# Attention stages of a two-model layer stack: turns one step behind the scores in two of three kinds of attention

## What is computed

```python
def diff_core(q, k, v, lam):                     # two maps a head, subtracted
    s = einsum('bqhid,bkhid->bhiqk', q, k) * DA ** -0.5
    p = softmax(s, axis=-1)
    w = p[:, :, 0] - lam * p[:, :, 1]
    return einsum('bhqk,bkhd->bqhd', w, v)

def mla_core(qn, qr, kn, kr, v):                 # scores are a sum of two products
    s = (einsum('bqhd,bkhd->bhqk', qn, kn) + einsum('bqhd,bkd->bhqk', qr, kr)) * MLA_SCALE
    return einsum('bhqk,bkhd->bqhd', softmax(s), v)

# window_gqa: scores of 256 context keys and of a band of up to 3 x 128 keys, softmax with a sink
# nsa_mixer: per query block o_c * gate_c + o_s * gate_s + o_w * gate_w, each a masked softmax @ values;
#   (31 compressed keys; selected keys; a window)
```

## Time and profile before

| | |
|---|---|
| median of 3 runs | 4268.4 us (4262.95 to 4271.06) |
| the profiled execution | 4266.7 us; its span 4264.5 us |
| PE busy | 3891.0 us, 91% |
| DVE busy | 2230.9 us, 52% |
| ACT busy | 1583.4 us, 37% |
| the eight attention calls together | 709.4 us (sum of their windows) |
| the six that are not combined | 553.0 us |

### The profile page before, as it was taken

One profiled execution on the slowest core, in us unless ns is written; L12 is line 12 of the kernel. 1 busy time (PEld: TensorE's weight loads), 2 busy tenths in 40 slices (PEclk: granted clock), 3 DMA queues, 4 the chain that ended last, 5 costly groups with the idle time before them and its releaser, 6 DMA issues. The chain is left out here.

```text
span 4264.5 us, 53701 instructions
## 1 busy us (share of the span) xinstructions
PE 3891.0 (91%) x19922; PEld 3027.8 (71%) x19922; DVE 2230.9 (52%) x3880; ACT 1583.4 (37%) x2699; POOL 318.7 (7%) x282
## 2 busy tenths in 40 slices
PE   4998979997999898999899899979889998988998
PEld 3875557776888787865666688856568886657886
DVE  6346567854553574364522556255555525565552
ACT  2235561112442453254611344243434424343431
POOL 0000001111000000100000100104010010401001
PEclk8999989998999999999999999989799999979999
DMA  4100005551222343100022233222023322202322
GB/s 173 57 31 19 1 17 175 195 185 54 96 96 100 107 163 114 65 23 19 1 83 86 79 97 97 95 71 80 11 79 95 102 89 85 75 21 79 98 98 80
DMA packets 86728, 350.82 MB, mean 82 GB/s; under 512 B 9520, under 2 KB 9648, under 8 KB 85680
## 3 DMA queue, kind: packets, MB, share of 16 engines
q1 hardware_dynamic: 72752, 298.53, 21.3%
q0 software_dynamic: 13824, 50.34, 3.5%
HBM read 346.73 MB, written 2.10 MB: 82 GB/s over the span
## 5 line engine op out<-in xcount | busy, mean ns | idle before, releaser
L493 DVE TENSOR_TENSOR split_low<-weight_ring,split_high 128x1024 fp32r<-128x1024 f32 (+1 forms) x456 | 606.2, 1330 | 893.3 <-ACT split_high L485 878.3
L485 ACT ACTIVATE split_high<-weight_ring 128x1024 fp32r<-128x1024 f32 (+1 forms) x474 | 524.7, 1109 | 1037.8 <-PE banks L1342 469.3
L1470 PE MATMUL banks<-normed_high,split_high 128*128 128x512 f32 (+1 forms) x1760 | 653.6, 371 | 77.9 <-DVE normed_low L432 37.9
L1470 PE MATMUL banks<-normed_low,split_high 128*128 128x512 f32 (+1 forms) x1760 | 651.2, 370 | 0.0
L1470 PE MATMUL banks<-normed_high,split_low 128*128 128x512 f32 (+1 forms) x1760 | 650.4, 370 | 0.0
L1470 PEld LDWEIGHTS banks<-normed_high,split_high 128*128 128x128 f32 x1760 | 334.4, 190 | 139.8 <-issue 83.6
L1470 PEld LDWEIGHTS banks<-normed_low,split_high 128*128 128x128 f32 x1760 | 334.5, 190 | 55.6
L1470 PEld LDWEIGHTS banks<-normed_high,split_low 128*128 128x128 f32 x1760 | 334.4, 190 | 55.2
L1342 PE MATMUL banks<-hidden_high,split_high 128*128 128x512 f32 (+1 forms) x880 | 325.1, 369 | 7.2 <-DVE split_low L493 7.2
L1342 PE MATMUL banks<-hidden_high,split_low 128*128 128x512 f32 (+1 forms) x880 | 324.4, 369 | 0.0
L1342 PE MATMUL banks<-hidden_low,split_high 128*128 128x512 f32 (+1 forms) x880 | 324.3, 369 | 0.0
(11 more groups left out here) (301 smaller groups left out, 6641.6 us busy)
## 6 DMA issues: line engine op xcount, KB each, us to landing
weight_ring<-in_up SPq DMA_DIRECT2D x220, 512.0 KB, 3.5
weight_ring<-in_down SPq DMA_DIRECT2D x80, 704.0 KB, 4.0
modulation_ring<-in_ada POOLq DMA_DIRECT2D x80, 512.0 KB, 4.5
weight_ring<-in_merge SPq DMA_DIRECT2D x48, 768.0 KB, 4.5
weight_ring<-in_inputs SPq DMA_DIRECT2D x36, 512.0 KB, 3.5
weight_ring<-in_out SPq DMA_DIRECT2D x32, 512.0 KB, 3.5
latents<-in_ada POOLq DMA_DIRECT2D x16, 512.0 KB, 4.6
weight_ring<-in_xbc SPq DMA_DIRECT2D x16, 512.0 KB, 3.6
```

What stands on the lines that cost most here:

```text
L485: act.activation(k.splits[0][:, (n0 + panel) % RING, 0:width], k.slot(n0 + panel)[:, 0:width], ACT.Copy).then_inc(k.high_ready.sem, 1)
L493: dve.tensor_tensor(k.splits[1][:, s, 0:width], k.ring[:, s, 0:width], k.splits[0][:, s, 0:width].bitcast(F32), ALU.subtract).then_inc(k.l ...
L1470: last = pe.matmul(sums(r, half), w, x, start=(c + j == 0), stop=(c == KT - 1 and j == 2))
```

## The change

`behind` is 2 for a combined call and 1 for the others. Where it is 2, nothing changes. Where it is 1:

- PE issues in iteration t: score(t), turn(t-1, 0), weigh(t-2), turn(t-1, 1).
- ACT issues: copy(t-1, 0), both exponentials of t, copy(t-1, 1).
- DVE issues: normalise(t-1) of both maps, then both maxima of t, then store(t-2).
- Each loop has one iteration less.

No instruction is added or taken away, and no buffer, bank or DMA is changed.

```diff
+    behind = 2 if combined else 1
...
-            for t in range(U + 3):
+            for t in range(U + behind + 1):
                 if t < U:
                     score(t)
-                if 2 <= t < U + 2:
-                    turn(t - 2, 0)
-                if t >= 3:
-                    weigh(t - 3)
-                if 2 <= t < U + 2 and per == 2:
-                    turn(t - 2, 1)
+                if behind <= t < U + behind:
+                    turn(t - behind, 0)
+                if t > behind:
+                    weigh(t - behind - 1)
+                if behind <= t < U + behind and per == 2:
+                    turn(t - behind, 1)
...
-            for t in range(U + 3):
+            def normalise_both(t):
+                if 0 <= t < U:
+                    normalise(t, 0)
+                    normalise(t, 1)
+
+            for t in range(U + behind + 1):
+                if behind == 1:
+                    normalise_both(t - 1)
                 if t < U:
                     maximum(t, 0)
                     maximum(t, 1)
-                if 1 <= t <= U:
-                    normalise(t - 1, 0)
-                    normalise(t - 1, 1)
-                if t >= 3:
-                    store(t - 3)
+                if behind == 2:
+                    normalise_both(t - 1)
+                if t > behind:
+                    store(t - behind - 1)
...
-            for t in range(U + 2):
-                if t >= 2:
-                    copy(t - 2, 0)
+            for t in range(U + behind):
+                if t >= behind:
+                    copy(t - behind, 0)
                 if t < U:
                     exponential(t, 0)
                     exponential(t, 1)
-                if t >= 2 and per == 2:
-                    copy(t - 2, 1)
+                if t >= behind and per == 2:
+                    copy(t - behind, 1)
```

## The result

The changed kernel takes 4242.6 us (median of 4 runs, 4238.85 to 4244.40), the kernel before took 4268.65 in the runs beside it (4262.95 to 4271.06). The ratio is 0.9939, with a 95% interval of 0.9924 to 0.9955: faster by 26 us, 0.6%. Forecast were 4255.2 and a range of 4246 to 4266. The sign was right, the size (13.2 us) was half of what came, and the time lies 3.4 us under the lower end.

What follows compares the result with a forecast made beforehand. PE was taken to bound latent calls, three engines with waits window calls, PE at clock 0.71 sparse calls. Latent -6.4, window -4.2, sparse +0.8, clock -3.4: -13.2 us, giving 4255.2 us, range 4246 to 4266.

Steps and rivals of the forecast that it cites:

- The prediction's own sign of being wrong: Wrong if the clock moved by over 13 us either way in these calls or the stages behind them.
- Drain: End of a call: one round of turn and weigh goes, saving 4.1 us latent, 3.2 and 3.6 window, 2.5 sparse.
- Fill: Start of a call: turn pair fills PE's 2.02 us hole, costing 0.9 us latent, 1.3 window, 1.3 sparse.
- Middle of the window calls: Loop through DVE and ACT stays 0.24 us a step shorter than what binds already: no cost.
- Order of the sparse calls: Drain -2.5, fill +1.3, DVE loop +1.6 a call (2.6 at full clock): +0.8 us for both calls.
- Clock of the first model: Latent and window calls: 12.8 us lost at half clock, a quarter regained by filling the second hole: -3.4 us.
- Clock of the sparse calls: No gain forecast; half of PE's load was called clock, and slow stretches only hid loop cost, 1.6 instead of 2.6 us.
- The combined calls: The two calls whose order is not changed were to stay at 89 and 67 us.
- Case 3: The clock doesn't fall at the start of calls: -22.6 us, 4245.8 us; chance 0.15.
- Case 2: DVE's order takes back the clock gain, full 2.6 us loss per sparse call: 4260 to 4265 us; chance 0.24.
- Case 4: Slower: the new loop's holes before scores keep PE at 1.2 GHz in window calls: 4280 us; chance 0.06.
- The rule of the Trainium skill: PE idling briefly and often between matmul groups oscillates between clock levels; a loop every step would cost more than its holes.

Runs made afterwards that it cites:

- fill_small_before: Kernel before, old order, plus unused 128x256 products behind score(0) and score(1) in latent, window and combined calls: 4251.75 us, ratio 0.9963.
- both_mixed: As both_after, but sparse calls keep the old order (turns two steps behind, maxima first): 4236.8 us, ratio 0.9930.
- both_after: Changed kernel plus unused products behind score(0) in latent, window and combined calls, and at several places in the sparse calls: 4235.3 us, ratio 0.9926.
- keep_before: Kernel before, old order, plus unused 128x256 products in the two sparse calls alone, 29 a call: 4256.6 us, ratio 0.9975.
- window_only: Kernel before with the new order in the two window calls alone, no products: 4257.0 us, ratio 0.9974.
- latent_only: Kernel before with the new order in the two latent calls alone, no products: 4259.7 us, ratio 0.9984.
- normalise_first: Changed kernel with turns two steps behind again in all calls, DVE still normalising t-1 ahead of the maxima of t: 4275.6 us, 1.0022 of the kernel before.
- maxima_first: Changed kernel, turns one step behind, but DVE takes the maxima of t ahead of normalise(t-1) everywhere: 4603.4 us, 1.0788 of the kernel before.

## Why the prediction was half right

Laid side by side, the six calls with the clock held by products are (us; "held" is fill_small_before for latent and window calls and both_mixed for the sparse, in the old order; both_after in the new; PEclk is 1.00 in the latent and window calls and 0.95 to 0.96 in the sparse ones):

| call | before | old order, held | new order, held | after |
|---|---|---|---|---|
| latent, layer 0 | 130.76 | 129.13 | 126.00 | 126.02 |
| window, layer 0 | 95.45 | 91.57 | 89.87 | 89.86 |
| latent, layer 1 | 107.39 | 105.75 | 102.62 | 102.62 |
| window, layer 1 | 73.16 | 70.42 | 68.37 | 69.58 |
| sparse, layer 0 | 74.84 | 68.74 | 69.52 | 69.93 |
| sparse, layer 1 | 72.99 | 69.02 | 69.52 | 70.20 |

The third number of a row less the second is the order's own share: -3.1, -1.7, -3.1, -2.0, +0.8 and +0.5, together -8.7. The rest of the 26.4 us, 17.7, is the clock's: 1.6, 3.9, 1.6, 1.5, 5.7 and 3.3. So the clock made two thirds of the gain, as far as one profile of each kernel can tell.

Against the sum of the prediction: the order in the latent calls -6.3 (forecast -6.4), in the window calls -3.7 (-4.2), in the sparse calls +1.3 (+0.8), and the clock -17.7 (-3.4). The terms of the order were right within 0.5 us; the term of the clock was a fifth of what it measured, and none of it was put on the sparse calls. The prediction's own sign of being wrong, a clock that moves by more than 13 us, came.

**Drain: right.** 4.1 us a latent call were forecast; 14.4 to 10.27 is 4.1.

**Fill: right.** (The pair of turns, 2.64 us, is 0.62 over the hole of 2.02, not 0.55; the 0.07 is the overlap with what follows, which the prediction took off without saying so.) score(2) begins 10.70 us after score(0) in place of 10.14, 0.56 later (0.55 forecast), and score(3) at 16.75. The old order had 17.41 there with a score at half clock in it, so 15.76 without the 1.65 of that (worked out from rows 4): 0.99 later, 0.9 forecast. For a latent call -3.2 was forecast and -3.1 measured, twice.

**Middle of the window calls: right.** Four steps take 15.77 us in the changed kernel (2066.78 to 2082.55, first scores). The 15.56 of the prediction is a mean over a stretch that still began with four shorter steps: 15.40 (2066.30 to 2081.70), then 15.72 (to 2097.42). So the new order adds 0.05 us in four steps, and the loop through DVE is covered. The calls at held clock lost 1.7 and 2.0 us against 1.9 and 2.3 forecast: from the end of the last score to the last store 3.1 and 3.5 less (3.2 and 3.6 forecast), and up to there 1.4 more in each (1.3).

**Order of the sparse calls: right in sign and place.** Forecast were +0.4 a call with part of the loop's cost hidden by the slow clock, +1.4 with all of it; with the clock held it is +0.8 and +0.5 (+1.5 by keep_before). The hidden part was counted too small: the prediction took 30.6 and 17 us at half clock, the longest stretch of each call, where the calls had 44.1 and 38.5 in all. DVE now waits where it was said to wait. The group of the first scaling of the 31-key steps, sparse call of layer 0, first after, then before (line, engine, operation, shapes, busy and mean; then idle time ahead and its releaser):

```profile
L1064 DVE SCALAR_TENSOR_TENSOR probs<-probs,tables 128x31 f32<-128x31 f32 x16 | 3.0, 187 | 6.9 <-ACT probs L1117 6.9
```

```profile
L1063 DVE SCALAR_TENSOR_TENSOR probs<-probs,tables 128x31 f32<-128x31 f32 x16 | 3.0, 185 | 0.0
```

The traces of both_mixed and both_after divide the sum, with the products in both. From the end of the last score to the last store it is 10.3 and 8.1 us: the drain gives back 2.2 (2.5 forecast). Up to the end of the last score the new order takes 3.0 and 2.7 us longer, for fill and loop together (1.3 + 2.6 forecast). Together these were priced 0.9 and 1.2 us too high; which of the two it was is open.

**Clock of the first model: the step that failed by its size.** The prediction put it as "The change fills the second hole but not the first, so I take a quarter, 3.4". Of what the four calls could give, 9.9 us by held clock (1.6 + 3.9 + 1.6 + 2.7), 8.7 came: nearly all. The stretch at 0.50 began behind the second hole in the rows, and that was the evidence; the first hole was given three quarters of the effect with no row for it. That hole can bring a fall: in the window call of layer 1 the slow stretch that is left begins right behind it, and is worth the 1.2 us by which this call is longer than with products in that place:

```profile
2034.70 1.13 PE L998 MATMUL banks<-window_keys,mixed 64*128 64x256 f32 x8 [0.66 <-PEq L987]
2037.42 2.50 PE L998 MATMUL banks<-window_keys,mixed 64*128 64x128 f32 x16 [1.58 <-DVE scalars L1053]
```

But it need not. In window_only the same call, with the same order and the same hole and no products, stays at 1.00 and takes 68.36 us:

```profile
2044.65 1.37 PE L999 MATMUL banks<-window_keys,mixed 64*128 64x128 f32 x16 [1.58 <-DVE scalars L1054]
```

And in latent_only the latent call of layer 1 falls for 3.4 us at its first hole, where in the changed kernel it doesn't. What decides between the two is open. So that nearly all came in the changed kernel was in part luck; with 8 of 12 calls of the new order free of any fall, a quarter was too little all the same. Also the 12.8 us said to be there were 9.9: half the busy time of the slow stretch was too much, 5.3 and 4.2 us for the 3.9 and 2.7 measured. That part of the slow work falls into waits is the likely reason.

**Clock of the sparse calls: the step that failed by its absence.** The sum priced the loop for the time in which PE is slow, and never asked if it would stay slow. Rows 2 had the clock at 0.71 there, the lowest of all, and rows 7 the longest stretch at 0.50, 30.6 us. The prediction saw it as load: it called half of PE's 64.46 busy us the clock. Some 40 of them lie in the stretches at 0.50, so that it is nearer a third (estimate: half of those 40). It is the largest single term of the result, 9.0 us. The windows of the slow first stretch of the call in the kernel before and of its last 7.85 us:

```profile
3015.13:3044.57 29.44, 27.50 (x122) 14.35 (x122) 18.60 (x110) 16.62 (x62) 0.00 (x0) 0.50 0.00 1
3082.12:3089.97 7.85, 6.05 (x41) 4.58 (x40) 0.29 (x1) 1.79 (x3) 0.00 (x0) 0.50 0.01 2
```

and in the changed kernel, the slow first stretch, the one behind it, and the last 16.7 us:

```profile
2994.60:3013.70 19.10, 17.28 (x79) 9.00 (x81) 12.56 (x78) 10.54 (x43) 0.00 (x0) 0.50 0.00 1
3014.00:3027.00 13.00, 10.26 (x79) 5.81 (x78) 10.76 (x47) 9.08 (x29) 0.00 (x0) 1.00 0.00 0
3047.80:3064.50 16.70, 12.64 (x110) 7.57 (x110) 10.52 (x43) 9.43 (x28) 0.00 (x0) 1.00 0.00 1
```

The first stretch ends 19.1 us into the call, where before it ended after 29.4 (rows 7 begin it ahead of the call). The call begins in it in both kernels, so the order does not prevent the fall; it brings the rise earlier. And a second thing: the fall at the end of the call, worth 7.85 us at half clock, does not come in the new order. In the sparse call of layer 1 the end is the whole of it: before, 3.4 us at half clock begin 54.9 us into the call and 7.8 at 65.2; after, there are none later than 53.3, while the first stretch is no shorter (17.1 us before, 19.2 after). All other profiles without products in these calls show the same for each order in layer 0 (29.3 to 29.4 us, and 19.1). Why the clock rises and holds at these places is not shown. That a turn and a weigh now stand between the first scores can't be all: in normalise_first, where they don't, the first stretch in layer 0 ends after 19.2 us too. The fall at the end, however, is there in normalise_first (at half clock for 3.4 us from 70.4 us into the call of layer 0, and from 68.5 to the end in layer 1), and so are three rounds of drain.

**The combined calls: forecast unchanged, and unchanged.** The 1.8 us of the first one are what the same instructions do from run to run, as said with the result. The same shows in keep_before: its latent calls, with nothing changed in them, took 136.66 and 113.64 us, at 0.94 and 0.91, against 130.76 and 107.39 in the profile of before. So the clock's share of single calls in the table above can be a few us off. The order's share is firmer, for windows at PEclk 1.00 agree within 0.03 us from kernel to kernel (126.00 to 126.03, 102.62, 89.86 to 89.88).

**The rivals.** Case 3, the clock that doesn't fall, with 4245.8 and 0.15, was the nearest: its mechanism is what happened in the four calls of the first model. That its number came within 3.2 us was luck, for its price was too high there and the sparse calls were missing. Case 2 had the loop in the sparse calls right and the clock wrong. Case 4 happened in another kernel than the one it was written for: maxima_first falls back to half the clock in its window calls again and again to their end, but there PE waits about 2.6 us in each step (2.58 and 2.65 in two of layer 0) and not some tenths. The rule of the Trainium skill behind it ("TensorE: Matmul & The Clock Gate", "A second HAM failure mode: psum-queue depth-cycling") was weighed only as a reason against the change. The runs show the other side of it: an order with fewer holes gave clock back.

## What to carry to other kernels

Where a timeline shows PE at half clock in a stage, a change of order has two prices: that of its waits at full clock, and that of the slow stretches it begins or ends. Write a term for each stage with a low PEclk, the stages with the lowest first. Where the hole that stands before a slow stretch is filled, count on most of the stretch and not on a quarter (8.7 of 9.9 us in four calls here), with the whole and nothing as ends, since the same instructions fell in one run and not in another. To part the two, hold the clock with products whose result nobody reads, sized from the trace to fit the hole, in both orders. And moving consumers one step closer needs the producer's engine to serve them first: each half of this change alone was slower than none, one by 9 us and one by 336. Compare such kernels call by call, and look at unchanged calls first: they moved by up to 6 us through the clock.

## What was not expected of the hardware

- A float32 product of 128x128 by 128x512 is two matmul instructions here and takes 0.91 us (four in 3.63); by 128x256 it is 0.50 (four in 1.99). I had assumed half.
- Half the clock costs less where PE has waits beside it: in the window call of layer 0, 13.6 us at 0.50 cost 3.9, 0.29 for each; in the latent calls, where PE has no slack, 3.4 us cost 1.6, 0.48 for each; in the changed sparse call of layer 0, 29.3 us in place of both_after's 5.5 made the call only 0.4 longer, but both_after has 29 products more in it, so this is no price of the clock alone.
- Extra work can make a stage faster: 29 products more, and the sparse call of the old order goes from 74.84 to 68.75 us.
